# The order of steps in two transformer blocks on one core: lanes woven by a rough clock per engine instead of by fixed rates

## What is computed

```python
for l in range(2):
    h = rmsnorm(x, mix_norm_g[l])
    a_b, a_c, a_x, q, k, v, c_in = split(h @ w_in[l])
    y_a = a_b * causal_conv(a_c * a_x, short_conv_w)              # 3 taps
    y_b = rmsnorm(diff_attention(rope(q), rope(k), v, lam))       # 4 heads, two softmaxes each
    c = glu(c_in + glu_b)
    y_c = silu(layernorm(causal_conv(c, conf_dw_w) + conf_dw_b))  # 31 taps
    x = x + concat(y_a, y_b, y_c) @ w_out[l]
    x = x + swiglu(rmsnorm(x, ffn_norm_g[l]))
# second block, once
h = rmsnorm(rmsnorm(x, final_norm_g), norm_mix)
oa = gated_deltanet(silu(causal_conv(h @ w_qkv)), ...)            # 8 heads, chunks of 64, a triangular solve per head
ob = chunk_band_attention(h @ w_qb, h @ w_kb, h @ w_vb, rel_bias) # 16 heads
y = sigmoid(h @ w_ga) * ((norm(oa) * silu(h @ w_za)) @ w_a_out) + sigmoid(h @ w_gb) * (ob @ w_b_out)
x = x + y @ w_o
x = x + memory_attention(rmsnorm(x), rmsnorm(mem))                # 4 heads, 256 memory rows
x = x + swiglu(rmsnorm(x)); out = rmsnorm(x)
```

## Time and profile before

| | |
|---|---|
| median of three runs | 2943.68 us (2941.9 to 2945.16) |
| profiled execution | 2936.2 us; its span, first to last instruction, 2934.9 us |
| mean granted clock of TensorE in it | 0.955 of full speed |
| busy: PE, DVE, POOL, ACT | 2717.8, 1235.8, 1058.5, 921.7 us |
| dense products, three passes of 1992 and of 912 matmuls (L1536) | mean 389 to 408 ns each, overlapped |
| DMA | 216.29 MB, 74 GB/s |

### The profile page before, as it was taken

How to read it: one execution, slowest core, us unless ns; L and a number is a source line. 1 busy time by engine, 2 the same in 40 slices (tenths; PEclk the granted TensorE clock), 3 DMA queues, 4 the chain that set the end, 5 groups by cost and what they waited for, 6 DMA issues and landing times.

```text
span 2934.9 us, 31943 instructions
## 1 busy us (share of the span) xinstructions
PE 2717.8 (93%) x13048; PEld 2190.6 (75%) x13048; DVE 1235.8 (42%) x2369; ACT 921.7 (31%) x1396; POOL 1058.5 (36%) x350
## 2 busy tenths in 40 slices
PE   7889999998889999988898999999989997999997
PEld 5667888886668888866677778767768885688886
DVE  7975211128863111257546564323443543311112
ACT  3242322232333212343223233215553333332222
POOL 3313544544224545432212122133213451254553
PEclk9999999999999999988899899889999998899999
DMA  4112223232112232221001011022212241122322
GB/s 155 44 44 75 97 84 111 87 107 72 43 44 100 87 108 86 85 88 43 29 15 44 15 44 44 29 86 87 80 51 87 88 142 43 58 87 93 100 87 78
DMA packets 36611, 216.29 MB, mean 74 GB/s; under 512 B 4080, under 2 KB 5232, under 8 KB 15856
## 3 DMA queue, kind: packets, MB, share of 16 engines
q1 hardware_dynamic: 36464, 214.23, 21.5%
HBM read 212.12 MB, written 2.10 MB: 73 GB/s over the span
## 4 chain that ended last, share of the span: by engine, by line
PE 77%; DVE 18%; ACT 2%; issue 2%; POOL 0%; DMA 0%; SPq 0%; DVEq 0%; ACTq 0%
PE PB L1536 60%; PE PB L1574 4%; DVE cc L2164 3%; PE PB L1538 2%; PE PB L1556 1%; PE PB L1548 1%; PE PB L1741 1%; DVE sm L2228 1%; PE PB L1716 1%; PE PB L1713 1%; DVE bp L2460 1%; PE PB L1725 1%; PE PB L1732 1%; PE PB L1703 1%; PE PB L1694 1%
## 5 line engine op out<-in xcount | busy, mean ns | idle before, releaser
L2527 POOL TENSOR_TENSOR WL<-WR,WH 128x2048 fp32r<-128x2048 f32 (+1 forms) x209 | 898.9, 4301 | 1151.2 <-ACT WH L1784 1151.2
L1536 PE MATMUL PB<-HH,WH 128*128 128x512 f32 x1992 | 813.4, 408 | 11.4 <-ACT HH L1796 8.9
L1536 PE MATMUL PB<-HL,WH 128*128 128x512 f32 x1992 | 791.0, 397 | 3.9 <-DVE HL L2071 3.7
L1536 PE MATMUL PB<-HH,WL 128*128 128x512 f32 x1992 | 519.0, 400 | 0.0
L1536 PEld LDWEIGHTS PB<-HH,WH 128*128 128x128 f32 x1992 | 382.9, 192 | 109.1 <-issue 17.6
L1784 ACT ACTIVATE WH<-WR 128x2048 fp32r<-128x2048 f32 (+1 forms) x209 | 371.6, 1778 | 264.8 <-PE PB L1536 256.9
L1536 PEld LDWEIGHTS PB<-HL,WH 128*128 128x128 f32 x1992 | 382.1, 192 | 92.3 <-DVE HL L2071 8.7
L1536 PEld LDWEIGHTS PB<-HH,WL 128*128 128x128 f32 x1992 | 375.1, 191 | 79.8 <-issue 4.0
L1536 PE MATMUL PB<-BH,WH 128*128 128x512 f32 (+1 forms) x912 | 354.0, 391 | 6.2 <-ACT BH L1809 4.8
L1536 PE MATMUL PB<-BL,WH 128*128 128x512 f32 (+1 forms) x912 | 352.5, 389 | 3.6 <-DVE BL L2079 2.7
L1536 PE MATMUL PB<-BH,WL 128*128 128x512 f32 (+1 forms) x912 | 221.3, 389 | 0.0
(11 more groups left out here) (328 smaller groups left out, 3102.7 us busy)
## 6 DMA issues: line engine op xcount, KB each, us to landing
WR<-in_w_gu SPq DMA_DIRECT2D x66, 1024.0 KB, 4.8
WR<-in_w_dn SPq DMA_DIRECT2D x48, 704.0 KB, 4.0
WR<-in_w_in SPq DMA_DIRECT2D x22, 1024.0 KB, 4.8
WR<-in_qkv SPq DMA_DIRECT2D x12, 1024.0 KB, 4.8
WR<-in_w_out SPq DMA_DIRECT2D x8, 1024.0 KB, 4.8
WR<-in_qk SPq DMA_DIRECT2D x8, 1024.0 KB, 4.9
WR<-in_za SPq DMA_DIRECT2D x4, 1024.0 KB, 4.8
WR<-in_ga SPq DMA_DIRECT2D x4, 1024.0 KB, 4.8
```

Source lines behind the costliest of these rows:

```text
L1536: ins = pe.matmul(out[:, 0:n], wt[:, k * cols + j * P:k * cols + (j + 1) * P], x[:, k, 0:n], start=first, stop=last)
L2527: g.tensor_tensor(m.WL[u % 2][:, 0:n], m.WR[u % 2][:, 0:n], f32(m.WH[u % 2][:, 0:n]), ALU.subtract).then_inc(sems["wlo"], 1)
```

## The change

Only the order of the list changes, with the size of the pieces in which dense tiles are issued and the choice of banks; no instruction's work does.

A class `Clock` holds a modelled time at which each of T (PE), V (DVE), A (ACT) and G (POOL) is free, and `when`, the modelled time of every signal. A table `ROUGH` gives each kind of step its engines and times, with a part that grows with the block number for attention steps; `pass_time` adds a step's time to its engines when the step is made. A dense piece costs 0.000445 us per column and matmul; a weight split 2.0 us on ACT and then 4.7 us on POOL. `weave` always takes the lane with the lowest modelled time: for a dense lane (marked True) that is PE's free time, for the others the end of their last step. A lane that can't go on is set just behind the earliest of the others. `beside`, `late` and all rates are gone; in the mixer `heads_in(0)` has become part of the dense lane. `Ring.take` takes the free room whose signals are known to come first, and `left` holds a lane back while no room is ready by the clock. `unit` with `fine` can yield after every two chunks, in place of after half of them.

```diff
+ROUGH = {
+    "score": [("T", 0.1, 0.43)], "smax": [("V", 0.6, 0.28)], "sexp": [("A", 0.7, 0.23)], "snorm": [("V", 0.5, 0.26)],
+    "strans": [("T", 0.1, 0.11), ("A", 0.2, 0.12)], "spv": [("T", 0.1, 0.22), ("A", 0.3, 0)], "hnorm": [("V", 0.8, 0)],
+    "ssq": [("A", 0.7, 0)], "ssq2": [("A", 1.3, 0), ("V", 0.8, 0)], "colsum": [("T", 0.9, 0)], "rsqrt": [("V", 2.3, 0)],
+    "diag": [("V", 0.8, 0)], "spread": [("T", 0.9, 0)], "settle": [("A", 0.7, 0)], "opv": [("A", 0.7, 0), ("V", 0.7, 0)],
+    "opg": [("A", 0.7, 0), ("G", 1.3, 0)], "tap": [("V", 0.8, 0)], "lnsum": [("T", 1.8, 0)], "lnsub": [("V", 1.5, 0)],
...
+    "rs2": [("V", 3.5, 0)], "nt": [("V", 0.9, 0)], "dq1": [("V", 1.3, 0)], "dq2": [("V", 2.5, 0)], "dq3": [("A", 1.3, 0)],
...
+    "p15": [("V", 1.0, 0)], "i1": [("V", 2.4, 0)], "i2": [("T", 0.5, 0), ("A", 0.7, 0)], "i3": [("T", 0.9, 0), ("A", 0.7, 0)],
+    "i4": [("T", 0.9, 0)], "i5": [("T", 0.9, 0)], "i6t": [("V", 0.8, 0)], "i6z": [("V", 0.8, 0)], "i7u": [("T", 0.9, 0), ("A", 0.7, 0)],
...
+class Clock:
+
+
+    def __init__(self):
+        self.free, self.when, self.lane, self.steps, self.weaving = {e: 0.0 for e in "TVAG"}, {}, 0.0, 0, False
...
+    def run(self, engine, us, after):
+        start = max(self.free[engine], after)
+        self.free[engine] = start + us
+        return self.free[engine]
...
-                return r
-        raise RuntimeError("all rooms are held")
+        rooms = [r for r in self.rooms if not r.held]
+        assert rooms, "all rooms are held"
+        r = min(rooms, key=lambda x: (self.clock.known(x.after), x.turn))
+        self.taken += 1
+        r.held, r.turn = True, self.taken
+        return r
 
     def left(self, n):
-        while sum(not r.held for r in self.rooms) < n + 1:
-            yield
+        while sum(not r.held for r in self.rooms) < n + 1 or self.clock.weaving and not self.ready():
+            yield
+
+    def ready(self):
+        now = max(self.clock.lane, self.clock.free["T"])
+        return any(not r.held and self.clock.known(r.after) <= now for r in self.rooms)
...
+            self.clock.when[self.last[engine]] = ends.get(engine, ends["end"])
         self.steps.append((kind, key, given))
+
+    def pass_time(self, kind, key, given):
+
+        c = self.clock
+        c.steps += 1
+        t, ends = max([c.known(x) for x in given.values()], default=0.0), {}
+        if kind != "mm" and c.weaving:
+            t = max(t, c.lane)
+        if kind == "mm":
+            u, j, part, start = key
+            op, ks, cols = given["op"], given["ks"][start:given["to"]], given["n"] if given["mode"] == "F" else self.units[u][3]
+            t = max(t, c.known(self.at("wlo" if part else "whi", u)), c.known([x for k in ks for x in (op.hi[k], op.lo[k]) if x]))
+            t = ends["T"] = c.run("T", len(ks) * (1 if part else 2) * cols * 0.000445, t)
+        if kind == "split":
+            t = c.known(self.unit_end[key[0] - 2].done) if key[0] >= 2 else 0.0
+            ends["A"] = c.run("A", 2.0, t)
+            ends["G"] = c.run("G", 4.7, ends["A"])
+            return {"end": t, **ends}
+        elif kind == "imask":
+            ends["G"] = c.run("G", 1.3, c.known(given["done"]))
+            return {"end": t, **ends}
+        elif kind != "mm":
+            n = key[-1] + 1 if kind in BY_BLOCK else 0
+            for engine, fixed, each in ROUGH.get(kind, ()):
+                t = ends[engine] = c.run(engine, fixed + each * n, t)
+        for tile in [given["tile"]] if "tile" in given else given.get("tiles", ()):
+            if "T" in ends:
+                tile.time = ends["T"]
+        if kind != "mm" and c.weaving:
+            c.lane = t
+        return {"end": t, **ends}
...
+def weave(clock, *lanes):
+
+
+    live = [[clock.free["T"], i, g, stream] for i, (g, stream) in enumerate(lanes)]
+    stuck = 0
     while live:
+        it = min(live)
+        clock.lane, clock.weaving, before = it[0], not it[3], clock.steps
+        try:
+            next(it[2])
+        except StopIteration:
+            live.remove(it)
+            stuck = 0
+            continue
+        if clock.steps > before:
+            it[0], stuck = clock.free["T"] if it[3] else clock.lane, 0
+        else:
+            it[0] = max(it[0], min([x[0] for x in live if x is not it], default=0.0)) + 0.05
+            stuck += 1
+            assert stuck < 100000, "no lane can go on"
+    clock.lane, clock.weaving = 0.0, False
...
                 done = 0
                 for i, k in enumerate(ks):
-                    if fine and (i == nk // 2 or part == 1 and i == 0):
+                    if fine and (i and i % 2 == 0 or part == 1 and i == 0):
                         if i > done:
...
-        taps = conv_taps()
-        beside(heads_in(0), (taps, 1))
...
-        weave((lane(heads_in(1), short_conv(), mixed()), 1.6), (lanes[0], 1), (late(2, lanes[1]), 1), (late(3, lanes[2]), 1),
-              (late(5, lanes[3]), 1), (taps, 1))
+        weave(clock, (lane(heads_in(0), heads_in(1), short_conv(), mixed()), True), *[(x, False) for x in lanes], (conv_taps(), False))
...
-        weave((products(), 1.3), (lane(gates(), preparations()), 1), (inversions(), 1), (scans(), 0.7), (gatings(), 1),
-              (rescale(), 1))
+        weave(clock, (products(), True), *[(x, False) for x in (lane(gates(), preparations()), inversions(), scans(), gatings(), rescale())])
...
-        weave((projections(), 0.6), (attend(0, 0, (0, 3)), 1), (late(1, attend(1, 0, (0, 3))), 1),
-              (late(3, attend(0, 1, (1, 2))), 1), (late(4, attend(1, 1, (1, 2))), 1))
+        weave(clock, (projections(), True), *[(attend(i, j, blocks), False) for j, blocks in ((0, (0, 3)), (1, (1, 2))) for i in range(2)])
...
-        weave((lane(*[queries(h) for h in range(4)], mixed()), 1), (lane(attend(0), attend(2)), 2),
-              (late(5, lane(attend(1), attend(3))), 2))
+        weave(clock, (lane(*[queries(h) for h in range(4)], mixed()), True), (lane(attend(0), attend(2)), False),
+              (lane(attend(1), attend(3)), False))
```

More of the change, by code:

```diff
@@ L283, in units, with known @@
     return out
+ROUGH = {
[23 rows of a table added]
+}
+BY_BLOCK = ("score", "smax", "sexp", "snorm", "strans", "spv", "bscore", "bsc", "bexp", "bnorm", "btrans", "bpv")
+class Clock:
+    def __init__(self):
+        self.free, self.when, self.lane, self.steps, self.weaving = {e: 0.0 for e in "TVAG"}, {}, 0.0, 0, False
+    def known(self, x):
+        if isinstance(x, Tile):
+            return max([x.time] + [self.known(y) for y in x.after])
+        if isinstance(x, tuple) and len(x) == 2 and isinstance(x[0], str) and isinstance(x[1], int):
+            return self.when.get(x, 0.0)
+        if isinstance(x, (list, tuple)):
+            return max([0.0] + [self.known(y) for y in x])
+        return 0.0
+    def run(self, engine, us, after):
+        start = max(self.free[engine], after)
+        self.free[engine] = start + us
+        return self.free[engine]
 class Room:
     def __init__(self, i):
-        self.i, self.held, self.after = i, False, []
+        self.i, self.held, self.after, self.turn = i, False, [], 0
     def free(self, *after):
@@ L337, in __init__ @@
         self.steps, self.count, self.value, self.last, self.tiles = [], {}, {}, {}, 0
+        self.clock, self.unit_end = Clock(), {}
     def step(self, kind, *key, **given):
+        ends = self.pass_time(kind, key, given)
         for signal in KINDS[kind]:
@@ L355, in finish @@
         self.last["T"] = ("tile", self.tiles)
+        self.clock.when[self.last["T"]] = tile.time
     def now(self, engines="VAGT"):
         return [self.last[e] for e in engines if e in self.last]
-def weave(*lanes):
-    live = [[g, n, 0.0] for g, n in lanes]
+def weave(clock, *lanes):
+    live = [[clock.free["T"], i, g, stream] for i, (g, stream) in enumerate(lanes)]
+    stuck = 0
     while live:
-        for it in list(live):
-            it[2] += it[1]
-            while it[2] >= 1:
-                it[2] -= 1
-                try:
-                    next(it[0])
-                except StopIteration:
-                    live.remove(it)
-                    break
-def beside(main, *lanes):
-    live = [[g, n, 0.0] for g, n in lanes]
-    for _ in main:
-        for it in list(live):
-            it[2] += it[1]
-            while it[2] >= 1:
-                it[2] -= 1
-                try:
-                    next(it[0])
-                except StopIteration:
-                    live.remove(it)
-                    break
+        it = min(live)
[13 more added lines that the diff above has]
+    clock.lane, clock.weaving = 0.0, False
 def drain(g):
@@ L400, in lane @@
         yield from g
-def late(n, g):
-    for _ in range(n):
-        yield
-    yield from g
 def order(m):
@@ L412, in order @@
     at, step, now = o.at, o.step, o.now
-    banks = [Room(i) for i in range(8)]
-    sbank, fbank = Ring(banks[0:2]), Ring(banks[2:8])
```

(12 more changed lines are left out.)

13 lines of the change are left out of this document (4 added, 9 removed), and 15 rows, old and new, of the table ROUGH.

## The result

The changed kernel takes 2966.05 us (median of 7, 2955.44 to 2979.77), the kernel before beside it 2942.42 us (7, 2936.35 to 2945.16): ratio 1.0087, 95% interval 1.0064 to 1.011. The forecast was 2844. The profiled execution of after took 2979.77 us with a span of 2978.4, at the upper end of its runs, so the spans differ by 43.5 us where the medians differ by 24.

A forecast was written before the change was run, and what follows sets the result against it. TensorE, busy 93% of 2934.9 us, was taken as the bound, with 301 us lost to gaps and clock in woven stages. Gains 28.5 + 43 + 0 + 5 + 14 + 9 = 99.5 us gave 2844 us, range 2755 to 2950.

The forecast's parts named there:

- Band, -14: Band attention: half of the 28.8 us lost to PE's gaps and the clock comes back, 14 us.
- Mixers, -28.5: Two mixers: DVE is the next limit, at most 28.9 + 28.0 us to win; half taken, 28.5 us.
- Rival 4: Woven stages: the clock doesn't know DVE steps blocked by POOL's subtractions; 40 us slower, 2984 us; 13%.
- Delta net and tail, -48: Delta net 1322 to 1680: half of 85.9 us, 43; scan tail: 5 of 33.6; entry and 1680 to 1873: 0.
- rival 2: Delta net's inversion chains set the pace, hops don't shorten; only mixers and band gain, 43 us, so 2901 us; 15%.
- Memory, -9: Memory attention: a quarter of 38.3 us, 9, as the last head's chain stands bare before the residual.
- Rival 5: Woven windows: alternating dense pieces and small products lowers TensorE's clock to 0.85; 16 us slower, 2960 us; 5%.

The follow-up runs named there:

- the cut: POOL subtracts only the first 16 columns of each weight block after the first two: kernel before 2804.41 us, changed kernel 2780.02 us.

## Why the prediction was wrong

**Band, -14: the step that failed.** It became +83. I wrote that instructions and their sizes stay, and priced the order by PE's gaps and the clock alone, so that an instruction's cost was its own in any order. Here it depends on the neighbour: the old order had the two heads wait for `projected` and then start in one round, so that their products ran side by side. Nothing in the rates says so; it came with the round. The windows give an estimate of the shares: at .81 the clock costs .19 x 316 = 60 us, in before .04 x 233 = 9, so about 51 of the 83 us are clock and 32 the rest, mostly products that have lost their neighbour. The runs give others, since slower products hide pauses: 17 or 18 us for the lost overlap with DVE's pauses left in (before 233, with overlap forbidden 250; after with whole-array products 251), 39 without pauses. 56 us go when the held-up steps go (316 - 260), 65 when the same products use the whole array (37 of them against half-array products that don't overlap either), 58 with pieces of four: the pause, the half-filled array and the fine pieces come together, and without any one of them most of the loss is gone (with pieces of four 12 more scores are paired too). Why the chip grants less clock in that case no run shows. The trace of before had the sign of the overlap: score matmuls 7 ns apart, each recorded with .69 us, so at the same time. I read only the stage's totals.

**Mixers, -28.5: nothing.** 192.4 and 191.8 became 191.7 and 192.7, DVE 86% and not over 90. I took half of DVE's idle time as recoverable by order. The limit was DVE's steps held up by POOL (taps of up to 5.09 us, 1.77 with the cut). The order meets them about as often: 12 and 11 steps over 1 us longer than their median in the two mixers of before, 11 and 11 in after, with 37 and 34 us of excess in each. With them gone the order is worth 19.4 us in the two: the mechanism was right, its condition wasn't met. Rival 4 had this mechanism, with the wrong result: in the mixers the blocks cost the old order as much as the new one.

**Delta net and tail, -48: -40.** Right in size by luck, since the parts were off and made up for each other. The inversions follow each other 59.3 us apart (1350.9 to 1766.3, against 65.4 in the earlier trace rows), so the chains did get shorter, which rival 2 ruled out, but by a tenth only. The stretch to the tail gave 18 us (1873 to 1855) where I had 43, the serial tail 17 where I had 5 (52 to 35 us), and the dense products behind it 5 where I had none.

**Memory, -9: nothing** (316 us in before and 317 in after from the gated output to the last feed-forward stage). Not followed up.

**Rival 5** said that the clock would fall, by alternation. It did fall, but not by that alone: with whole-array products the same alternation over the same banks ran at .97. The Trainium skill (TensorE: Matmul & The Clock Gate, A second HAM failure mode: psum-queue depth-cycling) tells of brief idles between groups of matmuls, and of a clock that goes up and down with them. The traces agree so far (behind after's pause at 1992 us it falls to .50 and comes back); but the same banks with 20.5 us of idle cost hardly any clock (.97) when the products filled the array, and those of after .81. The time of rival 4, 2984, lies near the profiled 2979.77 by accident: it has the loss in another stage.

What the forecast needed and lacked was a rival for a thing that the old order did without naming it. 28.5 + 14 + 9 = 51.5 us of expected gain that didn't come, 8 of the 48, and 83 of loss, make the 143 between 99.5 faster and 43.5 slower.

## What to carry to other kernels

Before an order is changed, look in the trace for instructions that run at the same time as a neighbour of their own engine (here score matmuls that start 7 ns apart, where the same eight, each alone, start 320 to 530 ns apart): that is an asset of the order, and a scheduler that costs each alone will break it. Issue such pairs from one lane. And take away what makes TensorE pause just ahead of work that fills half the array: here a stage with 24 us of pauses lost about 60 us more by the clock (.19 of 316 us).

## What I had not expected of the hardware

- Fine pieces of dense work alternating with lone matmuls on half of the array, after a pause of about 2 us: half clock for 17.0 us with no gap. The same with whole-array operands: full clock behind pauses of 1.9 us, and 3.4 us at half clock behind three of the four pauses of 2.3 us. So a kernel may get faster by multiplying more: V's products for both heads' columns, half of them unread, gave 2933.86 us against 2966.05.
- Slower matmuls can raise the clock: with overlap forbidden, .96 became .99 in before and .81 became .91 in after, since they cover late DVE steps.
- POOL's subtraction costs the kernel before 139 us (2943.07 to 2804.41) though POOL is busy 36% of the time and PE hardly ever waits for it: it holds up DVE. The Trainium skill (SBUF — State Buffer, SBUF: two separate sides) says that DVE and POOL share a port pair, that a DVE step with two SBUF inputs or in a 2-port mode needs it, and that one instruction holds it to its end. The taps of up to 5.09 us, with two SBUF inputs, agree; the normalization held up for 3.18 us has one and a scalar per partition, and whether it ran in a 2-port mode no row shows. The reciprocal of .15 us ran through beside the same subtraction.
